# Moving the transposed activations of the up projection: one view offset for all layers, or one for each layer and each half of the groups

## The reference

```
x = x + conv_ffn(rms_norm(x, ffn_norm[i]), w_up[i], conv_w[i], conv_b[i], w_down[i])

def conv_ffn(h, w_up, conv_w, conv_b, w_down):
    u = h @ w_up                                  # (256, 1024) @ (1024, 5632)
    u = causal depthwise convolution of width 3 over the tokens, plus conv_b
    gate, up = u[..., :D_FF], u[..., D_FF:]       # D_FF = 2816
    return (jax.nn.silu(gate) * up) @ w_down
```

## Time and profile before

| | |
|---|---|
| median of 3 runs | 1314.26 us (1313.72 to 1314.66) |
| the profiled execution's own time | 1313.94 us |
| its span, from first to last instruction | 1312.1 us |
| TensorE matmul busy | 1290.8 us, 98% of the span |
| TensorE weight load busy | 1095.7 us, 84% |
| VectorE / ScalarE / GpSimd busy | 1008.6 / 873.9 / 460.2 us |
| mean granted TensorE clock | 0.995 |

### The profile page before, as it was taken

The page is one execution under the profiler, slowest core; times in us unless marked ns, Lnnn a source line. Parts: engine busy times, 40 slices in busy tenths (PEclk is TensorE's granted clock), DMA queues, the critical chain, the costliest instruction groups (busy, mean ns, idle before and its releaser), DMA issues.

```text
span 1312.1 us, 22109 instructions
## 1 busy us (share of the span) xinstructions
PE 1290.8 (98%) x6964; PEld 1095.7 (84%) x6964; DVE 1008.6 (77%) x1603; ACT 873.9 (67%) x1567; POOL 460.2 (35%) x498
## 2 busy tenths in 40 slices
PE   6999999999999999999998999999999999999998
PEld 5888888888888888888886888888888888888887
DVE  5877899955777788885588788887476888888745
ACT  6777777744567777774467777775366776777533
POOL 3641245410275125552026315552014621555200
PEclk9999999999999999999999999999999999999999
DMA  7733555565564455556551365556455435555651
GB/s 263 233 113 130 176 193 192 192 215 169 198 229 152 139 178 189 192 193 216 169 185 57 111 212 189 189 191 212 160 196 193 144 113 182 189 191 192 213 172 64
DMA packets 64602, 232.39 MB, mean 177 GB/s; under 512 B 7472, under 2 KB 7600, under 8 KB 64528
## 3 DMA queue, kind: packets, MB, share of 16 engines
q1 hardware_dynamic: 61632, 221.35, 49.7%
q0 software_dynamic: 2896, 10.08, 2.3%
HBM read 230.35 MB, written 1.05 MB: 176 GB/s over the span
## 4 chain that ended last, share of the span: by engine, by line
PE 96%; DVE 2%; DMA 1%; ACT 1%; issue 0%; POOL 0%; SPq 0%; DVEq 0%
PE bank L1592 28%; PE bank L1898 25%; PE bank L1901 12%; PE bank L1568 7%; PE bank L1570 6%; PE bank L1569 6%; PE bank L1607 5%; PE bank L1739 2%; PE bank L1762 2%; PE bank L1578 2%; PE bank L1661 1%; DMA w_raw<-weights 1%; DVE w_lo L868 0%; DVE hT_both L922 0%; ACT w_hi L459 0%; PE bank L1686 0%
## 5 line engine op out<-in xcount | busy, mean ns | idle before, releaser
L868 DVE TENSOR_TENSOR w_lo<-w_raw,w_hi 128x1024 fp32r<-128x1024 f32 x418 | 544.0, 1320 | 112.4 <-ACT w_hi L459 111.4
L459 ACT ACTIVATE w_hi<-w_raw 128x1024 fp32r<-128x1024 f32 x418 | 430.1, 1052 | 139.9 <-PE bank L1592 107.4
L1898 PE MATMUL bank<-hT_both,w_hi 128*128 128x512 f32 x1408 | 439.8, 392 | 0.0
L1901 PEld LDWEIGHTS bank<-hT_both,w_lo 128*128 128x128 f32 x1408 | 264.4, 188 | 55.5
L1901 PE MATMUL bank<-hT_both,w_lo 128*128 128x256 f32 x1408 | 283.2, 279 | 0.0
L1553 POOL TENSOR_TENSOR gT_lo<-gate_c,gT_hi 128x256 f32 (+1 forms) x88 | 172.5, 1960 | 200.2 <-ACT gT_hi L820 200.2
L1898 PEld LDWEIGHTS bank<-hT_both,w_hi 128*128 128x128 f32 x1408 | 215.6, 188 | 4.0 <-issue 1.1
L1384 POOL TENSOR_SCALAR ssq<-ssq 128x1 f32<-128x1 f32 x24 | 12.7, 528 | 362.3 <-ACT tok L485 362.3
L1568 PE MATMUL bank<-w_hi,hT_both 128*128 128x512 f32 (+1 forms) x336 | 134.3, 400 | 3.2 <-DVE hT_both L922 2.2
L1570 PE MATMUL bank<-w_hi,hT_both 128*128 128x512 f32 (+1 forms) x336 | 130.6, 389 | 0.0
L1569 PE MATMUL bank<-w_lo,hT_both 128*128 128x512 f32 (+1 forms) x336 | 130.4, 388 | 0.0
(11 more groups left out here) (164 smaller groups left out, 1987.8 us busy)
## 6 DMA issues: line engine op xcount, KB each, us to landing
w_raw<-weights SPq DMA_DIRECT2D x418, 512.0 KB, 3.5
gain<-gains POOLq DMA_DIRECT2D x11, 512.0 KB, 4.5
rel<-rel_in POOLq DMA_DIRECT2D x8, 256.0 KB, 3.6
x<-x_in SPq DMA_DIRECT2D x4, 256.0 KB, 4.2
out<-x SPq DMA_DIRECT2D x4, 256.0 KB, 2.0
p_end<-p_in POOLq DMA_DIRECT2D x3, 256.0 KB, 5.2
consts<-consts_in POOLq DMA_DIRECT2D x1, 392.0 KB, 3.5
conv_sb<-conv POOLq DMA_DIRECT2D x1, 352.0 KB, 4.2
```

What stands on the lines that cost most here:

```text
L459: nc.scalar.activation(w_hi[:, slot, q * HALF:(q + 1) * HALF], w_raw[:, raw, :], ACT.Copy).then_inc(hi_ready, 1)
L868: nc.vector.tensor_tensor(w_lo[:, slot, cols], w_raw[:, half(q)[0], :], w_hi[:, slot, cols].bitcast(F32), ALU.subtract).then_inc(lo_ready, 1)
L1898: nc.tensor.matmul(up_banks(L, slot)[:, side, :], w_hi[:, *at(side)], hT_up[:, c, :, :], start=c == 0, stop=c == KC - 1, skip_group_check= ...
L1901: last = nc.tensor.matmul(up_banks(L, slot)[:, side, 0:SEQ], w_lo[:, *at(side)], hT_up[:, c, 0, :], start=False, stop=c == KC - 1, skip_gr ...
```

## The change

The offset of the view becomes a matter of the layer and of the half of the groups. Layers 0, 1 and 2 use offsets 32, 64 and 96 for groups 0 to 3, and 48, 80 and 112 for groups 4 to 7. Layer 3 keeps 16 for all groups. The writers (L501 and L928) and the readers (the two matmul lines of `up_unit`) use the same choice, so each reader finds what was written. All offsets are multiples of 16 values, 64 bytes, and all stay within the 128 spare values. The mixers' and gates' view stays at 0.

```diff
+UP_AT = ((32, 48), (64, 80), (96, 112), (16, 16))
...
-        hT, hT_up = hT_at(0), hT_at(16)
+        hT, hT_ups = hT_at(0), {at: hT_at(at) for at in sum(UP_AT, ())}
+        hT_up = lambda L, c: hT_ups[UP_AT[L][c // 4]]
...
-                    nc.scalar.activation((hT_up if n % 3 == 1 else hT)[:, 4 * b:4 * b + 4, 0, t * P:(t + 1) * P],
+                    nc.scalar.activation((hT_up(n // 3, 4 * b) if n % 3 == 1 else hT)[:, 4 * b:4 * b + 4, 0, t * P:(t + 1) * P],
...
-                    to = hT_up if n % 3 == 1 else hT
+                    to = hT_up(n // 3, 4 * b) if n % 3 == 1 else hT
...
-                                nc.tensor.matmul(up_banks(L, slot)[:, side, :], w_hi[:, *at(side)], hT_up[:, c, :, :],
+                                nc.tensor.matmul(up_banks(L, slot)[:, side, :], w_hi[:, *at(side)], hT_up(L, c)[:, c, :, :],
...
-                                last = nc.tensor.matmul(up_banks(L, slot)[:, side, 0:SEQ], w_lo[:, *at(side)], hT_up[:, c, 0, :],
+                                last = nc.tensor.matmul(up_banks(L, slot)[:, side, 0:SEQ], w_lo[:, *at(side)], hT_up(L, c)[:, c, 0, :],
```

## The result

| | before | after |
|---|---|---|
| median of 8 runs each | 1313.62 us | 1317.58 us |
| ratio | | 1.0037, 95% interval 1.0028 to 1.0045 |
| the profiled execution: time, span | 1313.94, 1312.1 us | 1319.38, 1317.6 us |

The changed kernel is slower by 0.37% (4.9 us by the ratio, 4.0 us by the medians). The forecast of no change was wrong, and the time lies outside the range.

The account below looks back on a forecast made before the run. TensorE, busy 98% of the span, was taken to bound the kernel. Readers 0 and writers 0 on 1313.94 gave 1313.9 us, with 0.3 us added back for the median 1314.2 us; range 1311.3 to 1317.0 us.

Parts of the forecast that it names:

- What bounds the kernel: Whole kernel: TensorE is busy 98% of the span, so an edit counts only by changing its issue pace or making it wait.
- 5.44 and 5.52 us a unit: Up projection: eight groups at the down projection's best rate take 5.44 us; an ordinary unit takes 5.52 us.
- layer 3 as the control: Up projection: layer 3 keeps offset 16; if layers 0 to 2 take another time, the address counts.
- Does the offset cause the 0.08 us?: Up projection: the ordinary unit's 0.08 us over best rate was put down to long and short matmuls in succession, not the address.
- The second argument: Down projection: its moving reads start at many places, yet one mean, 0.2267 us, holds over 76 matmuls.
- The equal windows of the four layers: Up projection: four windows alike to 0.1 us despite other engines' differing traffic, so that traffic doesn't show in TensorE's pace.
- The readers' term: Up projection matmuls in three layers: taken as 0, bounds 5.7 us less and 8.2 us more.
- the sign of being wrong: Up projection: any of the first three windows differing from 121.7 us by more than 0.9 us.
- reads that go worse: Up projection: offsets 32 to 112 fall on worse meetings of TensorE's two reads, 1316.9 to 1322.4 us; chance 0.08.
- The faster rival: Up projection: offsets at whole multiples of 128 bytes read better than 16, 1308.5 to 1311.6 us; chance 0.11.
- The writers' term: Up norm writes at L501 and L928, new addresses in three layers: 0, bounds -0.14 and +0.14 us.
- rule of two independent ports: TensorE reads moving operand and weights through two independent ports; by it both read rivals fall and the time is 1314.2 us.

Follow-up runs that it names:

- e2_uniform64: Changed kernel with one offset for all groups of a layer, 64, 80, 96, 112 values in layers 0 to 3; 5.573, 5.520, 5.573, 5.547 us a unit.
- e5_jump: Changed kernel with half-unit offsets (16, 80), (16, 32), (16, 48), (0, 64) in layers 0 to 3; 5.520, 5.573, 5.587, 5.573 us a unit.
- e1_uniform: Changed kernel with one offset for all groups of a layer, 0, 16, 32, 48 values in layers 0 to 3; 5.573, 5.520, 5.573, 5.547 us a unit.
- e9_hTshift: Changed kernel with offset 0 everywhere and 16 unused values between the weights and all tensors behind them; up projection 5.520 us a unit, 1328.02 us in all.
- e6_all512: Changed kernel with w_lo matmuls at 512 columns too, offsets 0, 16, 32, 48 in layers 0 to 3; 7.253, 7.325, 7.437, 7.467 us a unit.

## Why the prediction was wrong

**What bounds the kernel** was right: no wait and no other engine took part, and a few nanoseconds a matmul went straight into the time. The 5.44 and 5.52 us a unit, read from starts, and the use of layer 3 as the control held.

**The step that failed** is the one under "Does the offset cause the 0.08 us?": a pattern that repeats after three groups in one unit and after two in another can't come from the address, "so the lost time belongs to the succession of long and short matmuls". The groups lie 2,048 bytes apart, a whole multiple of the 256 bytes that count (e2_uniform64, e5_jump), so the position is the same in every group. It is a constant of the whole projection, and the pattern is what the engine settles into under that constant. The first unit shows it directly: in layer 0 of e1_uniform, in the same order and with only the position changed to 0, the pairs are 0.351 and 0.342 us apart in turn, a repeat of two and not of three. A repeat of three speaks against an address that varies from group to group, and says nothing about one that doesn't. What the runs showed in place of that step is the position modulo 256 bytes and its change within a unit, together 0.067 to 0.074 us a unit in the three layers. The second argument failed likewise: the down projection reads at many places, but all are at one distance modulo 256 bytes from its stationary operand, and e9_hTshift, which changes that distance, moves its mean from 226.8 to 233.3 ns. The equal windows of the four layers were rightly read against other engines' traffic; they had nothing on TensorE's own two reads.

**The readers' term**, taken as 0, measured 4.35 us, inside the bounds of -5.7 and +8.2 us. The first three windows lie 1.1 to 1.5 us over 121.7, past the 0.9 us that the prediction named as the sign of being wrong. The rival that came true, "reads that go worse", had 0.08. It came true with more than its number: it was told as worse meetings of the moving reads with the weight reads, and the distance between those two is what the runs found. Its size splits by the paces of e1_uniform. In layer 0 the settled pace rose by 0.074 us: 0.040 because offsets 32 and 48 have 5.573 and 5.547 us by themselves, 0.034 because the position changes twice in a unit. In layer 1 (64 and 80, positions 0 and 16) it is 0.027 and 0.040. Layer 2 has layer 0's positions and its 5.594 us. 21 ordinary units by 0.074, 0.067 and 0.074 make 4.5 us; the first units gave 0.14 us back, which leaves the 4.35.

**The faster rival** supposed that whole multiples of 128 bytes are better. Both, 0 and 32, are worse in this order (5.573 against 5.520); when all matmuls are long (e6_all512), 0 is better than 16 and 32 is worse. No offset tried beat 16.

**The writers' term**, 0 with 0.14 us either way, held: the pairs take 1.12 and 1.29 us again. In layer 0 of e1_uniform, where the up norm is written at offset 0, ScalarE's pair takes 1.11 us, against 1.09 in the gate's norm. So its being slower in the up norm is not due to the offset; the PSUM banks remain as an untested cause.

```profile
138.28 1.11 ACT L503 ACTIVATE hT_both<-bank 128x512 fp32r<-128x512 f32 x2
```

**The Trainium skill's rule of two independent ports** (SBUF — State Buffer, Who interferes with whom) was used to say that both rivals about reads fall. The runs go against what was drawn from it: with nothing but the distance between moving and stationary operand changed, the same matmuls take 226.7 or 233.3 ns (e6_all512, and e9_hTshift's down projection), so the pace hangs on where its two reads stand to each other. The measurement decides.

**What stays open** is the mechanism. Shown is that the distance modulo 256 bytes sets the pace, that changing it between matmuls costs more, and that matmul lengths and order decide which distance is best. That reads of weights and activations collide in SBUF is the nearest reading of this, but no run shows a collision, and no rule found here foretells the twenty paces. A pad that gives mixers, down and up projection each their own best distance was not tried beyond what the view offset already does.

## What to carry to other kernels

Where TensorE is the bound, the distance between the moving and the stationary operand's SBUF addresses modulo 256 bytes is a tuning parameter: up to 0.16 us of 5.5 (2.9%) between the best and the worst place here, at no cost in instructions. Keep one position for all matmuls of a loop, try multiples of 16 values (64 bytes) first, which stayed at or under 5.573 us in this kernel's order, and try them separately for each order of matmul lengths. After inserting any small tensor, read the start-to-start spacing of the big matmul loops again, since a 64-byte pad between weights and activations cost this kernel 14 us. And before an argument from a pattern excludes a cause, ask whether that cause could be constant over the pattern.

## What the hardware showed that was not expected

- Most settled paces are exact: 5.520 us again and again over units, layers and kernels, while DMA and the other engines differ. Offsets 18, 28 and 56 don't settle to one value.
- All-long matmuls: 226.7, 228.9, 232.4 and 233.3 ns each at offsets 0, 16, 32 and 48 values.
- Most settled units lie at 5.44 us plus whole multiples of 13.3 ns: 6 at offset 16, 8 at 8, 36 and 48, 10 at 0, 4 and 32, 12 at 12, 20 and 24, 14 at 40, 16 at 2, 10, 14, 44 and 60, 18 at 52.
- The first unit, in which lengths alternate one by one, ranks the offsets otherwise: 5.63 us at 0 and 5.73 at 16, from the starts in e1_uniform.
